# Dummy products on TensorE in three waits of a streaming encoder layer

## The chip, the cores and the metric

The kernel runs on one core of one Trainium2 chip, as one launch. The metric is the device time of the launch in microseconds (us); lower is better. The chip's other cores are idle.

## The reference, cut to what matters

One post-LN encoder layer is computed for 256 prompt frames and 64 sample frames together (320 tokens, model width 1024, float32). Cut to the branch in which the change lies:

```python
z = x @ w_in
q, k, v, u, vs, ga, gb = jnp.split(z, SPLIT_POINTS, axis=-1)
# A: chunked attention, 8 heads x 64, learned relative bias
sc = einsum('bnqhd,bnkhd->bhqk', q, k) * (A_HEAD_DIM ** -0.5) + bias
pr = jax.nn.softmax(sc, axis=-1)
oa = einsum('bnhqk,bnkhd->bnqhd', pr, v)
# B: spatial gating, 8 groups x 64 channels over 128-position chunks
un = jax.nn.gelu(u)
vn = layer_norm(jax.nn.gelu(vs), mlp_ln_g, mlp_ln_b)
ob = un * (tril(w_s[g]) @ vn + b_s[g])
mix = jax.nn.sigmoid(ga) * (oa @ w_branch_a) + jax.nn.sigmoid(gb) * (ob @ w_branch_b)
x = layer_norm(ALPHA * x + mix @ w_out, ln1_g, ln1_b)
# then 64 routed experts (top 8) and a shared one, a second norm, a gated embedding
```

## The kernel before

The kernel is written engine by engine: each engine has its own list of instructions, in the order in which the source has them, and semaphores tie the lists together. There is no planner; what an engine does next is what stands next in its list, and a wait holds back all that stands behind it on that engine.

The stages in order of time are: the input norm; the input projection in tiles of 128 columns (`products`, L1340, run by the loops of `project`); token-major copies, scores and softmax in between; the mixing product of branch B (L1418); the turned probabilities and the attention of branch A; the branch products with `w_branch_a` and `w_branch_b`, then with `w_out` (all L1340 again); the transposed result (L1493), the embedding product (`embed`, L1500), the first norm and the router; the routed experts in 16 steps of four experts (L1593, L1609, L1564, L1623); and the second norm and the output gate (L1704 to L1728).

The place of the change is the stretch between the last input projection and the first branch product. There TensorE's list reads:

- The mixing products (L1418): 24 products into PSUM banks 0 to 3; the last raises `mix_ps`.
- A wait for `prob_ready` 3, which VectorE raises after it has divided the last group of probabilities (L1007).
- `turn_probs(0)`: 12 transposes (L1426, L1428, L1431, L1434) into banks 4 to 6; the last raises `probT_ps`.
- A wait for `mix_ready` 1, which VectorE raises after it has read the mixing products from banks 0 to 3, added the bias rows (L1035, L1038) and multiplied by the activated `u` (L1040). `turn_probs(1)` writes banks 0 to 2, so it may not start before.
- `turn_probs(1)`: 12 transposes.
- `attend(0)`: its waits are `probT_act` 1 (ScalarE's copy of banks 4 and 5, L699) and `probT_dve` 1 (VectorE's copies of bank 6, L1049 and L1050); then 12 products (L1450 to L1460) into bank 7. Between `attend(0)` and `attend(1)` stands `turn_probs(2)`, behind `attend(1)` stands `turn_probs(3)`, and `attend(2)` and `attend(3)` follow. `attend` of an odd pair writes bank 3.
- A wait for `oa_ready` 4 (VectorE, L1054, after ScalarE's L705), and then the branch products.

SyncE's list has one gate in this stretch: it waits for `oa_ps` 4, which the last `attend` raises, before it loads the embedding's weights (L456 to L458) and, behind those, expert weights and the next pieces of the weight ring.

`ident` is the 128 x 128 identity in float32 that the transposes use. Bank 7 is written and read in earlier stages, and by `attend(0)` and `attend(2)`.

Of the kernel before, what the change touches and what calls it, by code (L numbers as in the profile page):

```python
# [34 lines left out]
P = 128  # L35
# [11 lines left out]
def trunk_step(nc, x_prompt, x_sample, cache_k, cache_v, p_prompt, p_sample, ln_in_g, ln_in_b, w_in,  # L47
# [30 lines left out]
    with ExitStack() as ctx:  # L78
        def sb(name, shape, dt=F32):
            return ctx.enter_context(nc.sbuf_tensor(name, shape, dt))  # L80
# [22 lines left out]
        ident = sb("ident", [P, P])  # L103
# [18 lines left out]
        PS = ctx.enter_context(nc.psum_tensor("PS", [P, 8, 512], F32))  # L122
# [1187 lines left out]
        def _(pe):  # L1310
# [67 lines left out]
            for h in range(HEADS):  # L1378
                par, i = h % 2, h // 2
# [20 lines left out]
            for w in range(2):  # L1400
                if w:
                    pe.wait_ge(score_ready, 4)
                for h in range(4 * w, 4 * w + 4):
                    par, i = h % 2, h // 2
                    for c, (key, n) in enumerate(((ckT[64 * par:64 * par + 64, i, :], 256), (head(K0, h, slice(256, TOK)), DH))):
                        ins = pe.matmul(PS[0:DH, 4 + 2 * par + i % 2, 256 * c:256 * c + n], query(h, 2), key,
                                        start=True, stop=True)
# [6 lines left out]
            for t in range(3):  # L1414
                n = ROWS[t]
                for g in range(8):
                    par = slice(64 * (g % 2), 64 * (g % 2) + 64)
                    ins = pe.matmul(PS[par, g // 2, cols(t)], vn[0:n, t, 64 * g:64 * g + 64], wsT[0:n, g, 0:n],  # L1418
                                    start=True, stop=True)
            ins.then_inc(mix_ps, 1)  # L1420

            def turn_probs(j):
                b = 4 if j % 2 == 0 else 0
                for e in range(2):
                    h = 4 * e + j
                    pe.transpose(PS[:, b + e, 0:P], prob0[:, h, :], ident[:, :])  # L1426
                    for c in range(2):
                        pe.transpose(PS[:, b + e, P * (c + 1):P * (c + 2)], prob1[:, h, P * c:P * (c + 1)], ident[:, :])  # L1428
                for e in range(2):
                    for c in range(2):  # L1430
                        pe.transpose(PS[:, b + 2, 192 * e + 64 * c:192 * e + 64 * c + 64], probs[:, 4 * e + j, P * c:P * (c + 1)],  # L1431
                                     ident[0:DH, 0:DH])
                for e in range(2):
                    ins = pe.transpose(PS[0:DH, b + 2, 192 * e + 128:192 * e + 192], probs[:, 4 * e + j, 256:TOK], ident[0:DH, 0:DH])  # L1434
                ins.then_inc(probT_ps, 1)

            def attend(j):
                pe.wait_ge(cache_loaded, 32)
                pe.wait_ge(probT_act, j + 1)
                pe.wait_ge(probT_dve, j + 1)  # L1440
                bank = 7 if j % 2 == 0 else 3
                if j >= 2:
                    pe.wait_ge(oa_ready, j - 1)

                for product in range(6):
                    for e in range(2):
                        rows, c, o = slice(64 * e, 64 * e + 64), slice(64 * (2 * j + e), 64 * (2 * j + e) + 64), 192 * e
                        pt, ps = probT[:, j, e, :], probT[:, j, 2, :]
                        if product == 0:
                            pe.matmul(PS[rows, bank, 0:P], v_tok[:, 0, c], pt[:, backwards(0, P)], start=True, stop=True)  # L1450
                        if product == 1:
                            pe.matmul(PS[rows, bank, P:2 * P], v_tok[:, 0, c], pt[:, backwards(P, 2 * P)], start=True, stop=False)
                        if product == 2:
                            pe.matmul(PS[rows, bank, P:2 * P], v_tok[:, 1, c], pt[:, backwards(2 * P, 3 * P)], start=False, stop=True)
                        if product == 3:
                            pe.matmul(PS[rows, bank, 256:TOK], cv[:, 0, c], ps[:, backwards(o, o + 64)], start=True, stop=False)
                        if product == 4:
                            pe.matmul(PS[rows, bank, 256:TOK], cv[:, 1, c], ps[:, backwards(o + 64, o + 128)], start=False, stop=False)
                        if product == 5:
                            ins = pe.matmul(PS[rows, bank, 256:TOK], v_tok[0:DH, 2, c], ps[0:DH, backwards(o + 128, o + 192)], start=False, stop=True)  # L1460
                ins.then_inc(oa_ps, 1)

            pe.wait_ge(prob_ready, 3)
            turn_probs(0)
            pe.wait_ge(mix_ready, 1)
            turn_probs(1)
            for j in range(4):
                attend(j)
                if j < 2:
                    turn_probs(j + 2)  # L1470
# [52 lines left out]
            for k in range(KD):  # L1523
                for wp, xp in ((0, 0), (0, 1), (1, 0)):
                    at = (wp * KD + k) * NE
                    ins = pe.matmul(PS[:, 6, 0:TOK], marks[:, at:at + P], xT[:, xp, k, :], start=(k == 0 and (wp, xp) == (0, 0)),  # L1526
                                    stop=(k == KD - 1 and wp == 1))
# [250 lines left out]
```

## Time and profile before

| | |
|---|---|
| time, median of 3 runs | 872.2 us (872.04 to 872.93) |
| the profiled execution's own time | 874.54 us |
| its span, first to last instruction | 872.5 us |
| TensorE (PE) busy | 819.9 us, 94% of the span |
| VectorE (DVE) busy | 381.5 us, 44% |
| ScalarE (ACT) busy | 269.1 us, 31% |
| chain that ended last | PE 86%, DVE 6%, DMA 3%, ACT 2% |
| mean granted TensorE clock | 0.986 of full speed |

The profile has one row for each group of instructions. A product of float32 operands shows as two records on PE and two weight loads on PEld; a transpose shows as one of each.
### The profile page before, as it was taken

The page shows a single profiled execution, that of the slowest core. Times are in us where ns is not written, and L with a number is a line of the kernel's source. Part 1 is how long each engine was busy: PE and PEld are TensorE (multiplying, and loading weights), DVE is VectorE, ACT ScalarE, POOL GpSimd, SP SyncE. Part 2 cuts the span into 40 slices and gives each one's busy share as a digit, 9 for nine tenths or more (in the row PEclk, how much of TensorE's full clock was granted, in tenths as well). Part 3 has the DMA queues.
Part 4 walks back from the last instruction along what each step waited for, and adds up shares of the span by engine and source line. Part 5 has one row for each costly group of instructions (what it writes and reads, how often), then busy time and mean ns, then how long its engine had stood idle before and what let it go on. Part 6 is the DMA issues. An engine that isn't in the chain of part 4 may idle for free.

```text
span 872.5 us, 13427 instructions
## 1 busy us (share of the span) xinstructions
PE 819.9 (94%) x4927; PEld 565.9 (65%) x4927; DVE 381.5 (44%) x846; ACT 269.1 (31%) x501; POOL 33.3 (4%) x50
## 2 busy tenths in 40 slices
PE   3999899889888999999999999999999999998887
PEld 2999799779877845555554654644645555553577
DVE  6435575737557834234224314414413423422674
ACT  2334466733434532211211211210220221120443
POOL 2001100000000320000000000000000000000000
PEclk9999999979999999999999999999999999999989
DMA  7596424427763059999999999999999999999001
GB/s 229 173 257 191 157 97 144 163 100 260 290 200 145 1 225 423 388 383 411 398 384 383 423 387 380 424 385 382 425 387 383 423 386 385 411 396 363 13 1 60
DMA packets 66041, 249.01 MB, mean 285 GB/s; under 512 B 5856, under 2 KB 37040, under 8 KB 41440
## 3 DMA queue, kind: packets, MB, share of 16 engines
q1 hardware_dynamic: 64848, 244.70, 71.3%
q0 software_dynamic: 1152, 3.95, 1.6%
q8 instruction: 16, 0.26, 0.1%
q14 instruction: 9, 0.07, 0.0%
q10 hardware_dynamic: 16, 0.02, 0.0%
HBM read 245.62 MB, written 3.03 MB: 285 GB/s over the span
## 4 chain that ended last, share of the span: by engine, by line
PE 86%; DVE 6%; DMA 3%; ACT 2%; SPq 1%; issue 1%; ACTq 0%; PEldq 0%; DVEq 0%
PE PS L1593 26%; PE PS L1340 20%; PE PS L1609 13%; PE PS L1623 9%; PE PS L1564 9%; PE PS L1714 4%; DMA weight_ring<-in_w_in_dram 1%; DMA weight_ring<-in_shared_w_dram 1%; PE PS L1602 1%; DVE xs L903 1%; PE PS L1572 1%; DMA expert_ring<-in_ln_in_b_dram 1%; PE PS L1526 1%; DVE xs L913 1%; DVE parts L1184 1%
## 5 line engine op out<-in xcount | busy, mean ns | idle before, releaser
L1593 PE MATMUL PS<-expert_ring,z 128*64 128x512 f32 x1024 | 223.7, 594 | 0.7 <-DVE z L1228 0.7
L1340 PE MATMUL PS<-parts,split 128*128 128x320 f32 x1344 | 202.3, 313 | 5.5 <-DVE parts L1068 3.3
L1340 PEld LDWEIGHTS PS<-parts,split 128*128 128x128 f32 x1344 | 200.4, 191 | 6.8 <-PEq L1483 3.5
L1593 PEld LDWEIGHTS PS<-expert_ring,z 128*64 128x64 f32 x1024 | 72.1, 137 | 139.7 <-issue 139.4
L1609 PE MATMUL PS<-expert_ring,z 128*64 128x512 f32 x512 | 113.7, 596 | 0.8 <-ACT z L788 0.8
L939 DVE TENSOR_TENSOR split<-weight_ring,split 128x512 fp32r<-128x512 f32 x106 | 73.8, 705 | 90.6 <-ACT split L635 90.3
L1224 DVE TENSOR_TENSOR split<-PS,split 128x512 fp32r<-128x512 f32 x64 | 44.3, 692 | 142.3 <-ACT split L793 141.9
L635 ACT ACTIVATE split<-weight_ring 128x512 fp32r<-128x512 f32 x112 | 69.9, 631 | 114.6 <-PE PS L1340 98.5
L784 ACT ACTIVATE z<-PS 128x256 f32<-128x256 f32 x32 | 12.3, 384 | 277.0 <-PE PS L1593 277.0
L1211 DVE SCALAR_TENSOR_TENSOR z<-PS,z 128x256 f32<-128x256 f32 x32 | 15.5, 485 | 183.1 <-ACT z L784 183.1
L1564 PEld LDWEIGHTS PS<-marks,parts 128*128 128x128 f32 x640 | 78.7, 191 | 14.0 <-issue 13.8
L1564 PE MATMUL PS<-marks,parts 128*128 128x256 f32 x640 | 85.0, 287 | 0.0
L1623 PEld LDWEIGHTS PS<-marks,split 128*128 128x128 f32 x512 | 75.2, 188 | 14.1 <-issue 13.0
L1623 PE MATMUL PS<-marks,split 128*128 128x320 f32 x512 | 80.5, 314 | 0.0
L1609 PEld LDWEIGHTS PS<-expert_ring,z 128*64 128x64 f32 x512 | 34.6, 136 | 66.2 <-issue 65.9
L793 ACT ACTIVATE split<-PS 128x512 fp32r<-128x512 f32 x64 | 38.2, 598 | 81.3 <-PE PS L1609 81.3
L1228 DVE TENSOR_TENSOR z<-z,PS 128x320 f32<-128x320 f32 x128 | 54.3, 484 | 11.7 <-PE PS L1623 10.1
L769 ACT ACTIVATE z<-PS 128x512 f32<-128x512 f32 x64 | 38.2, 597 | 47.8 <-PE PS L1564 47.8
L1714 PE MATMUL PS<-parts,split 128*128 128x320 f32 x192 | 31.9, 329 | 5.9 <-DVE parts L1274 4.8
L1714 PEld LDWEIGHTS PS<-parts,split 128*128 128x128 f32 x192 | 30.9, 205 | 6.7 <-issue 5.3
L1314 PE MATMUL PS<-ident,xs 128*128 128x128 f32 (+1 forms) x48 | 7.8, 326 | 15.7 <-DVE xs L913 15.7
L1165 DVE TENSOR_TENSOR marks<-z 128x256 fp32r<-128x256 f32 x51 | 18.6, 420 | 6.5 <-PE PS L1564 6.0
(225 smaller groups left out, 526.0 us busy)
## 6 DMA issues: line engine op xcount, KB each, us to landing
expert_ring<-in_exp_w_dram SPq DMA_DIRECT2D x192, 1024.0 KB, 10.0
weight_ring<-in_w_in_dram SPq DMA_DIRECT2D x36, 512.0 KB, 4.4
weight_ring<-in_w_out_dram SPq DMA_DIRECT2D x8, 512.0 KB, 4.4
expert_ring<-in_ple_w_gate_dram SPq DMA_DIRECT2D x2, 2048.0 KB, 10.2
weight_ring<-in_w_branch_a_dram SPq DMA_DIRECT2D x4, 512.0 KB, 3.6
weight_ring<-in_w_branch_b_dram SPq DMA_DIRECT2D x4, 512.0 KB, 4.6
weight_ring<-in_shared_w_dram SPq DMA_DIRECT2D x4, 512.0 KB, 7.2
xs<-in_x_prompt_dram SPq DMA_DIRECT2D x2, 512.0 KB, 4.5
```

The costliest lines, as they stand in the source:

```text
L635: nc.scalar.activation(split[:, 2 * (place % 2) + half, 0, :].rearrange("p (k n) -> p k n", k=4), raw, ACT.Copy)\
L769: nc.scalar.activation(xgT[:, 2 * g:2 * g + 2, :].rearrange("p k s -> p (k s)"), PS[:, g % 2, :], ACT.Copy)\
L793: nc.scalar.activation(ysplit[:, j, 0, 512 * half:512 * half + 512], PS[:, 5 + half, :], ACT.Copy)\
L939: nc.vector.tensor_tensor(parts[:, 1, :, :], raw, parts[:, 0, :, :].bitcast(F32), ALU.subtract).then_inc(w_low, 1)
L1224: nc.vector.tensor_tensor(ysplit[:, j, 1, c], PS[:, 5 + half, :], ysplit[:, j, 0, c].bitcast(F32), ALU.subtract).then_inc(y_low, 1)
L1228: nc.vector.tensor_tensor(accT[:, q, :], accT[:, q, :], PS[:, SCAT_BANK[q], 0:TOK], ALU.add)\
L1340: ins = pe.matmul(out, w[:, wp, :], xT[:, xp, k0 + k, :], start=(start and k == 0 and (wp, xp) == (0, 0)), stop=(stop and k == 3 and wp == 1))
L1564: ins = pe.matmul(PS[:, g % 2, 256 * k:256 * k + 256], xrows[:, part, t, 2 * g + k, :], pick[:, t, :], start=(t == 0 and part == 0), stop= ...
L1593: ins = pe.matmul(PS[c, 2 + j, :], xgT[:, k, P * j + 64 * e:P * j + 64 * e + 64], w13(j, e, k), start=(k == 0), stop=(k == KD - 1))
L1609: ins = pe.matmul(PS[c, 5 + half, :], hidT[:, j, k, c], w2(j, e, k, half), start=(k == 0), stop=(k == 1))
L1623: ins = pe.matmul(PS[:, SCAT_BANK[q], 0:TOK], ysplit[:, j, part, P * q:P * (q + 1)], scat[:, j, 0:TOK], start=(j == 0 and part == 0), stop ...
L1714: ins = pe.matmul(PS[:, tile % 2, 0:TOK], w[:, wp, :], xT[:, xp, k, :], start=(k == 0 and (wp, xp) == (0, 0)), stop=(k == KD - 1 and wp == 1))
```

## The change

A helper `fill(n)` puts n products into TensorE's list, each of which multiplies the identity by itself into the first 128 columns of PSUM bank 7. They wait for nothing, raise no semaphore, and nothing reads what they leave there: `attend(0)`, the next writer of that bank, starts its sums afresh. Four stand ahead of the wait for `prob_ready`, seven between `turn_probs(0)` and the wait for `mix_ready`, and five between `turn_probs(1)` and `attend(0)`, whose own waits follow. No wait is removed, added or moved, and the lists of the other engines are the same.

```diff
                 ins.then_inc(oa_ps, 1)
 
+
+            def fill(n):
+                for i in range(n):
+                    pe.matmul(PS[:, 7, 0:P], ident[:, :], ident[:, :], start=True, stop=True)
+
+            fill(4)
             pe.wait_ge(prob_ready, 3)
             turn_probs(0)
+            fill(7)
             pe.wait_ge(mix_ready, 1)
             turn_probs(1)
+            fill(5)
             for j in range(4):
                 attend(j)
                 if j < 2:
```

## Rows read from the trace of the kernel before

**Rows 1.** The page's 40 equal slices of the span: granted TensorE clock in tenths.

```profile
PEclk9999999979999999999999999999999999999989
```

**Rows 2.** Stretches: length, busy (records) of PE, PEld, DVE, ACT, POOL; PE clock; DMA.

```profile
172.30:175.70 3.40, 1.78 (x18) 1.33 (x18) 2.03 (x4) 2.90 (x3) 0.00 (x0) 1.00 0.28 97
175.70:179.10 3.40, 1.33 (x13) 1.32 (x14) 2.49 (x5) 1.31 (x2) 0.00 (x0) 0.51 0.00 0
179.10:182.50 3.40, 3.40 (x30) 2.66 (x28) 0.49 (x1) 0.44 (x1) 0.00 (x0) 0.50 0.00 0
182.50:185.90 3.40, 3.40 (x30) 3.14 (x30) 1.10 (x3) 1.25 (x2) 0.00 (x0) 0.50 0.02 5
185.95:190.78 4.83, 3.34 (x56) 2.74 (x55) 1.60 (x4) 1.69 (x3) 0.00 (x0) 1.00 0.11 14
```

**Rows 3.** Timeline of PE: start, length, instruction, records, idle before and its releaser.

```profile
168.10 2.58 PE L1418 MATMUL PS<-expert_ring 128*64 128x128 f32 x48 [1.20 <-ACT z L676]
171.37 0.33 PE L1426 MATMUL PS<-ident,expert_ring 128*128 128x128 f32 x1 [0.69 <-DVE expert_ring L1007]
...
172.47 0.27 PE L1434 MATMUL PS<-ident,expert_ring 64*64 64x64 f32 x2
174.36 0.33 PE L1426 MATMUL PS<-ident,expert_ring 128*128 128x128 f32 x1 [1.62 <-DVE z L1040]
...
177.81 0.70 PE L1450 MATMUL PS<-expert_ring 128*64 128x128 f32 x4 [2.07 <-DVE expert_ring L1050]
...
180.13 0.47 PE L1426 MATMUL PS<-ident,expert_ring 128*128 128x128 f32 x1
...
182.43 0.69 PE L1450 MATMUL PS<-expert_ring 128*64 128x128 f32 x4
...
184.74 0.47 PE L1426 MATMUL PS<-ident,expert_ring 128*128 128x128 f32 x1
...
186.43 0.27 PE L1434 MATMUL PS<-ident,expert_ring 64*64 64x64 f32 x2
186.63 0.44 PE L1450 MATMUL PS<-expert_ring 128*64 128x128 f32 x4
...
187.93 0.44 PE L1450 MATMUL PS<-expert_ring 128*64 128x128 f32 x4
...
190.78 3.49 PE L1340 MATMUL PS<-parts,split 128*128 128x320 f32 x22 [1.49 <-PEq L1473]
```

**Rows 4.** Timelines of DVE and ACT: what the waits of this stretch are for.

```profile
168.50 2.82 DVE L1007 TENSOR_TENSOR expert_ring<-expert_ring,srec 64x2560 f32<-64x2560 f32 x1
172.82 1.49 DVE L1040 TENSOR_TENSOR z<-expert_ring,z 128x1280 f32<-128x1280 f32 x1
177.39 0.27 DVE L1050 COPY expert_ring<-PS 64x128 f32<-64x128 f32 x1
175.52 1.49 ACT L699 ACTIVATE expert_ring<-PS 128x768 f32<-128x768 f32 x2
```

**Rows 5.** Chain of the end, two pieces: float32 products of full height, start and length.

```profile
270.71 1.08 PE PS L1500 x4
817.13 4.32 PE PS L1704 x16
```

**Rows 6.** Timeline of PEld: one load of 128 columns at the full clock.

```profile
171.37 0.14 PEld L1426 LDWEIGHTS PS<-ident,expert_ring 128*128 128x128 f32 x1 [0.82 <-DVE expert_ring L1007]
```

**Rows 7.** Timeline of SyncE's queue: the first load behind the gate on `oa_ps`.

```profile
189.34 0.37 SPq L456 DMA_DIRECT2D expert_ring<-in_ple_w_proj_dram  x1
```

**Rows 8.** Stretches elsewhere, columns as in rows 2: two lower-clock ones and two beside them.

```profile
222.50:223.45 0.95, 0.95 (x7) 0.95 (x8) 0.95 (x3) 0.25 (x1) 0.95 (x7) 1.00 0.68 248
223.50:226.85 3.35, 3.35 (x15) 3.35 (x14) 2.33 (x6) 0.63 (x1) 0.35 (x2) 0.50 1.02 355
...
831.10:837.80 6.70, 5.88 (x22) 5.91 (x23) 5.64 (x12) 2.79 (x6) 0.00 (x0) 0.50 0.00 0
...
254.70:257.50 2.80, 2.80 (x26) 2.80 (x27) 2.10 (x3) 0.57 (x2) 1.28 (x1) 1.00 0.02 6
```

## The prediction

> **What bounds the kernel now.** TensorE is busy for 94% of the span and carries 86% of the chain that ended last, so nearly every microsecond is a matter of how fast it works and where it has to wait. The first view to read is the page's line of granted clocks: all of the span runs near full speed but for a few slices, and the lowest of them, the ninth, is the place of the change [rows 1]. The second is a table of stretches around that place: the clock is 1.00 until 175.70, 0.50 from there to 185.90, and 1.00 again from 185.95 [rows 2]. Ahead of the fall TensorE was busy for only 1.78 of 3.40 us; while the clock was low it was first idle and then busy without a gap for 6.80 us. The third view is TensorE's own timeline, which names the idle pieces: 0.69 us until the last probabilities are divided, 1.62 us until the mixing result is free, and 2.07 us until the turned probabilities of the first pair are copied [rows 3]. VectorE's and ScalarE's rows say that these three waits end with their work, not with TensorE's [rows 4]. So the waits themselves can't be shortened by anything that TensorE does. What can change is the clock at which `attend` and `turn_probs` run behind them, and from 177.81 on each of them follows the one before with no wait between.
>
> **What the low clock costs.** The same two routines stand in the timeline at both levels, so the price is a difference of starts [rows 3]. One `attend` at the full clock takes 187.93 - 186.63 = 1.30 us. `attend(0)` takes 180.13 - 177.81 = 2.32 and `attend(1)` 184.74 - 182.43 = 2.31, so they lose 1.02 and 1.01 us. One `turn_probs` at the full clock takes 172.47 - 171.37 = 1.10 to its last two transposes, and those take 186.63 - 186.43 = 0.20 until the next routine starts: 1.30. `turn_probs(2)` takes 182.43 - 180.13 = 2.30 and loses 1.00; `turn_probs(3)`, in which the clock rises, takes 186.63 - 184.74 = 1.89 and loses 0.59. The sum is 1.02 + 1.00 + 1.01 + 0.59 = 3.62 us. All of it lies on the path: the branch products at 190.78 wait for the last `attend` and its two copies.
>
> **What is late next if it goes.** With the full clock from 177.81 on, `turn_probs(2)` ends at 177.81 + 2.60 = 180.41 and `turn_probs(3)` at 183.01. `attend(2)` follows at 183.01 and `attend(3)` at 184.31. The latter needs ScalarE's copy of `turn_probs(3)`: two copies take 1.49 us [rows 4], one thus about 0.75, which ends near 183.9, 0.4 us ahead of need. So no copy becomes the bound, and the branch products start at 187.16. SyncE's loads behind the gate on `oa_ps` begin at 189.34, right behind the last `attend` [rows 7], and move with it; DMA is all but idle in this stretch (0.00 to 0.11 of its time from 175.70 on [rows 2]), so there is no backlog that would hold them.
>
> **What the dummies cost.** Sixteen products of 128 columns are added, that is 32 records. No row has such a product, so its price is bounded. From below: float32 products of full height pass at 1.08 / 4 = 0.27 us a record for 320 columns, in two different places [rows 5]. By columns that is 0.27 x 128 / 320 = 0.108 us a record, 0.22 us a product, with the weight load hidden. From above: if the load of 128 columns, 0.14 us [rows 6], were not hidden at all, a record would take 0.108 + 0.14 = 0.25 and a product 0.50 us. I take 0.22, because the transposes are the nearest rows in shape, and theirs pass at 1.10 / 10 = 0.11 us each, load included [rows 3]. Nothing excludes a little more; a price below the bound of the stream has no row that would support it.
>
> With a price p the order of TensorE's list gives 170.68 + 4p for the end of the first four, if they start only where the mixing row ends (168.10 + 2.58). Then come 1.30 for `turn_probs(0)`, 7p, 1.30 for `turn_probs(1)`, and 5p. At p = 0.22 the first four end at 171.56, 0.19 us behind the release at 171.37; the seven at 174.40, 0.04 behind the release at 174.36; the five at 176.80, 1.01 us ahead of the release at 177.81. So `attend(0)` starts where it did, and the dummies cost nothing: VectorE and ScalarE, whose work ends the waits, hide them. What is queued behind them on TensorE is `turn_probs(0)` and `turn_probs(1)`; those are needed by ScalarE's copies at 175.52 and about 176.27, and would now end at about 172.9 and 175.7. The cover is used up where 170.68 + 2.60 + 16p = 177.81, at p = 0.28. The whole gain is used up where it is 177.81 + 3.62, at p = 0.51. The upper bound of 0.50 would leave 181.28, a delay of 3.47 and a gain of 0.15.
>
> The page "TensorE: Matmul & The Clock Gate" of the Trainium skill has a rule that speaks for the upper bound (Part 3: Packing small matmuls, "What overlaps and what doesn't"): a weight load overlaps with running products only when they use different groups of rows, and the dummies all use all 128. By that rule the sum would be the 872.05 that the upper bound gives. The rows of float32 products don't bear it out: theirs use all rows too, and 0.27 us leaves little room for a load of 0.14 beside the stream [rows 5, 6].
>
> **Whether they hold the clock.** This is the step that no row settles. For it: the fall came behind a stretch that was about half idle [rows 2], and with the dummies TensorE's idle time between 168.10 and 177.81 shrinks from 0.69 + 1.62 + 2.07 = 4.38 us to about 1.0. Against it: being busy is not enough in itself. From 179.10 to 182.50 TensorE was busy without a gap, with much of it transposes, and the clock did not rise; from 182.50 to 185.90, with more of `attend` in it, it did [rows 2, 3]. The dummies are products, like `attend`, not transposes, and they are asked to hold a clock, not to raise it; 2.80 us of transposes alone passed at 1.00 elsewhere [rows 8].
>
> **The rivals.**
>
> The dummies don't hold the clock. Then the five run at half speed, 5 x 0.44 = 2.20 us from 175.70 to 177.90, 0.09 us too late: 872.3. A milder form is a fall a little later, in the second half of the routines, that gives back part of the 3.62: 870.6 to 872. The page just named has a rule for that (Part 4: PE-mode transpose): transposes don't count as activity in the same way. The trace agrees in part: the transposes from 179.10 on did not raise the clock, but those at 254.70 kept it. Chance 0.11.
>
> More is gained than the sum. The kernel falls to the lower level in other places, and the moment isn't tied to an instruction: one fall comes at 223.50, after TensorE has been at work again for the 0.95 us from 222.50 [rows 8]. If the work arrives there 3.6 us earlier, a fall can be missed or shortened. The first costs 3.35 / 2 = 1.7 us, the second 5.88 / 2 = 2.9 us, of which about half might go: 865.3 to 867. Chance 0.16.
>
> The same chance of timing works the other way: a new fall, above all around 254.70, where transposes stand on the path behind a wait. Doubling the first eight of 24 costs about 1 us, all of them 2.80 us: 869.6 to 871.4, centre 870.9. Chance 0.06.
>
> Slower than before: the dummies don't pass in a stream, load and product of each record take turns. That is 0.14 + 0.33 = 0.47 us a record by single rows [rows 3, 6], 0.94 a product. `attend(0)` would start at 170.68 + 2.60 + 16 x 0.94 = 188.3, 10.5 us late, and the sum is 872.2 + 10.5 - 3.6 = 879.1. It decides from p = 0.51, and shows as over 0.2% from p = 0.62. Every run of float32 products in the trace speaks against it. Chance 0.03.
>
> **How the numbers follow.** The profiled execution took 874.54 us for a span of 872.5, 2.3 us more than the median of the timed runs, so the sum is 874.54 - 3.62 = 870.9 for such an execution, and 872.2 - 3.62 = 868.6 against the median. That is the forecast, with a chance of 0.64. The range of 865.5 to 871.2 takes in the rival with more gain, nearly all of the one with a new fall and a dummy price of up to 0.44 us; it leaves out the dummies that hold nothing and the slower case. A measurement of this kernel can tell about 0.2%, 1.7 us, from no change. Faster by more than that are the forecast and the larger gain, 0.80; within it the rivals of no hold and of a new fall, 0.17; slower 0.03.
>
> **What would show it.** In the profile of the changed kernel: a clock of 1.00 from 172 to 187; all four `attend` at 1.30 us and `turn_probs` at 1.30; a row of dummies at 0.11 us a record; `attend(0)` still released by L1050 near 177.8; the branch products near 187.2, and the chain behind them earlier by the same amount. The prediction is wrong if the clock still falls before 187, if the dummies' row reaches beyond 177.8, or if the falls of rows 8 come elsewhere or last longer.

## The result, and the profile after

The changed kernel is slower: 877.56 us (median of 8 runs, 874.53 to 880.84) against 872.88 us (869.93 to 874.81, 8 runs), a ratio of 1.005 with a 95% interval of 1.0026 to 1.0074. The profiled execution took 876.47 us for a span of 874.5 us, against 874.54 and 872.5 before. Forecast were 868.6 us and a range of 865.5 to 871.2. Ratios and medians are of executions within 1.5% of the fastest of their kernel; one alone was slower than that, of the kernel with 224 waits below (892.96 us).

In the stretch of the change the trace shows what was predicted. TensorE's timeline of the changed kernel there (columns as in rows 3; L1466 is the line of the dummies):

```profile
169.06 1.16 PE L1466 MATMUL PS<-ident 128*128 128x128 f32 x8
170.06 0.27 PE L1426 MATMUL PS<-ident,expert_ring 128*128 128x128 f32 x1
...
171.30 1.83 PE L1466 MATMUL PS<-ident 128*128 128x128 f32 x14
172.97 0.27 PE L1426 MATMUL PS<-ident,expert_ring 128*128 128x128 f32 x1
...
174.22 1.38 PE L1466 MATMUL PS<-ident 128*128 128x128 f32 x10
176.25 0.44 PE L1450 MATMUL PS<-expert_ring 128*64 128x128 f32 x4 [0.66 <-DVE expert_ring L1050]
...
177.55 0.33 PE L1426 MATMUL PS<-ident,expert_ring 128*128 128x128 f32 x1
...
178.85 0.44 PE L1450 MATMUL PS<-expert_ring 128*64 128x128 f32 x4
...
180.15 0.33 PE L1426 MATMUL PS<-ident,expert_ring 128*128 128x128 f32 x1
...
182.75 0.44 PE L1450 MATMUL PS<-expert_ring 128*64 128x128 f32 x4
185.61 6.57 PE L1340 MATMUL PS<-parts,split 128*128 128x320 f32 x43 [1.49 <-PEq L1481]
```

`attend` and `turn_probs` take 1.30 us each from start to start, and `attend(0)` is still released by VectorE's copy, now after 0.66 us of idle time instead of 2.07. From `attend(0)` to the branch products there are 185.61 - 176.25 = 9.36 us; before there were 190.78 - 177.81 = 12.97 [rows 3]. The gain is 3.61 us.

The whole stretch ran at the full clock, which the first row of this table of stretches shows (columns as in rows 2). The other rows are for later:

```profile
172.00:187.00 15.00, 12.86 (x162) 11.31 (x161) 6.49 (x14) 6.33 (x10) 0.00 (x0) 1.00 0.11 31
...
783.30:788.90 5.60, 0.00 (x0) 0.00 (x0) 1.68 (x5) 0.00 (x0) 0.00 (x0) 0.68 1.02 418
789.00:792.00 3.00, 3.00 (x8) 1.02 (x10) 0.00 (x0) 0.00 (x0) 0.00 (x0) 0.50 0.24 96
218.80:222.00 3.20, 3.20 (x14) 3.20 (x13) 1.85 (x4) 0.63 (x1) 0.00 (x0) 0.50 1.06 383
249.50:252.80 3.30, 3.16 (x15) 3.16 (x16) 1.72 (x2) 0.75 (x3) 1.27 (x1) 0.50 0.00 0
833.20:839.80 6.60, 5.95 (x22) 5.98 (x23) 5.59 (x12) 2.62 (x5) 0.00 (x0) 0.50 0.00 0
```

The loss is 600 us further on. The chain of the end, in the changed kernel, where the loop over the expert steps ends and the last step begins (start, length, what; "issue" is time in which the engine waited for nothing that the profile shows):

```profile
782.74 0.50 DVE z L1228
783.24 5.76 issue
788.99 15.53 PE PS L1601 x64
```

The same place in the kernel before:

```profile
787.92 0.50 DVE z L1228
788.42 0.19 issue
788.61 13.97 PE PS L1593 x64
```

The changed kernel arrives 787.92 - 782.74 = 5.18 us earlier. 3.61 us of that are the change. The rest was there ahead of it: `attend(0)` starts at 176.25 instead of 177.81, because the first 144 projection products took less time in this execution (first line) than in the one before (second line):

```profile
21.90 21.39 PE PS L1340 x144
21.76 23.10 PE PS L1340 x144
```

Then TensorE stands still for 5.76 us instead of 0.19, which takes back 5.57. The clock falls during that stand [the rows of 783.30 and 789.00 above], and the products behind it take 15.53 instead of 13.97 us, another 1.56. The balance is -5.18 + 5.57 + 1.56 = +1.95 us, the difference of the two spans.

While TensorE stands, no semaphore is waited for. What the DMA queues moved in those 5.6 us (packets, MB, share of 16 engines):

```profile
q1 hardware_dynamic: 315, 2.32, 100.4%
q8 instruction: 1, 0.02, 1.1%
```

The packet of 16 KB on q8 is an instruction fetch. In the trace the packets of that queue come 12 times up to about 370 us, none during the remaining 13 rounds of the loop, and then at 786.2 and 790.1 us; in the kernel before, at 791.4 and 794.9, behind the restart at 788.6 and not ahead of it. In both the first of them comes about 3 us behind the end of the loop (783.24 and 788.42).

### The profile page after: what moved, and what is told of

Same layout as the page of the kernel before. It is cut to its first block, busy times and chain, and to the rows that moved or that the text cites. A ratio compares the mean times of both kernels' runs of the same rounds, so it can differ in the third digit from the quotient of the medians.

```text
span 874.5 us, 13491 instructions
## 1 busy us (share of the span) xinstructions
PE 819.6 (94%) x4959; PEld 564.9 (65%) x4959; DVE 381.6 (44%) x846; ACT 268.8 (31%) x501; POOL 33.3 (4%) x50
## 4 chain that ended last, share of the span: by engine, by line
PE 87%; DVE 5%; ACT 2%; DMA 2%; issue 2%; SPq 1%; ACTq 0%; PEldq 0%; DVEq 0%
PE PS L1601 26%; PE PS L1340 20%; PE PS L1617 13%; PE PS L1631 9%; PE PS L1572 9%; PE PS L1722 4%; DMA weight_ring<-in_w_in_dram 1%; PE PS L1610 1%; DMA expert_ring<-in_ln_in_b_dram 1%; PE PS L1580 1%; DVE xs L903 1%; DVE xs L913 1%; DVE parts L1184 1%; PE PS L1508 1%; PE PS L1716 1%
```

## The experiments

**The theory.** TensorE's loop over the expert steps (391 instructions) is followed by a conditional block for overflow rounds, which these inputs never run; it is jumped over. By the built program's counts the code behind the jump begins 403 instructions behind the loop's last one. If instructions come in blocks, it matters in which block that code begins. The 16 dummies are 64 instructions (two loads and two products each), all ahead of the loop, and move everything behind by 64. Theory A: they push the code behind the jump across the edge of a block, into one that has not been fetched. Theory B: the stall comes with the dummies at work, or with arriving earlier.

The Trainium skill has this mechanism in "Runtime: NRT & Kernel Launch" (Instruction fetch mechanics): instructions are refilled in blocks of 16 KiB, 256 of them, in sequence, and a branch whose target is outside of what is loaded waits for a fetch. The trace agrees on the size of a block (packets of 16 KB) and has a fetch in the stand of 5.76 us.

**Never-executed instructions alone.**

```diff
             with pe.If(more > 0):
+                for _ in range(128):
+                    pe.wait_ge(const_ready, 1)
                 with pe.Fori(0, more) as r:
```

Two such waits make one instruction, so these are 64, in the block that is jumped over.

> The kernel before, with 64 instructions added inside TensorE's list in the conditional block that is jumped over behind the expert loop; they are never executed. Theory A (place of the code: the jump behind the expert loop lands in a 16 KB instruction block that has not been fetched when the code behind it lies 64 instructions further on): the stall of the changed kernel appears at the end of the expert loop, 5.8 us against 0.2 us, with a low clock behind it that costs about 1.5 us more, so about 872.9 + 7 = 880 us; the low clock around 176 to 186 stays as in the kernel before. Theory B (the stall comes from the dummies at work or from arriving earlier at the end of the loop): nothing that is executed has changed, so 872.9 us and no stall.

Measured: 880.34 us, ratio 1.0082 (1.0065 to 1.0098). The chain at the end of the loop:

```profile
783.35 5.57 issue
788.92 15.80 PE PS L1593 x64
```

Nothing that runs was changed, and the kernel is 7.2 us slower (873.16 beside it). The two lines account for it: (5.57 - 0.19) + (15.80 - 13.97) = 7.2 us. Dummies at work can't be the cause. This execution arrived as early as the changed kernel, so its trace alone doesn't exclude the other half of theory B; two traces below do, one that arrives at 794.40 and stands, and one that arrives at 782.14 and doesn't.

**The same 64 at the head.** The waits stand ahead of the first transposes, and are executed.

> The kernel before, with 64 waits on a semaphore that has long been raised put at the head of TensorE's list, where it idles for 16 us before the first norm; no dummies. Theory A: all code behind lies 64 instructions further on, as in the changed kernel, so the stall of about 5.8 us appears behind the expert loop: about 880 us, with the low clock around 176 to 186 kept. Theory B: 872.9 us, no stall.

Measured: 881.08 us, ratio 1.0098 (1.0073 to 1.0122), and a stall at the same place, as theory A has it:

```profile
784.17 5.75 issue
```

The jump here is as long as in the kernel before, so its length is not what counts.

**Moving the code on by 224 instead.** 160 waits at the head of the changed kernel, and 224 at the head of the kernel before.

> The changed kernel, with 160 waits on a raised semaphore at the head of TensorE's list, so that with the 64 instructions of the dummies all code behind lies 224 instructions further on than before; by the counts of instructions the jump behind the expert loop then ends in the block after the one it starts from, as in the kernel before. Theory A: no stall (0.2 us there), and the gain of the prediction is left: 872.9 - 3.6 = 869.3 us. Theory B: the stall stays, 877.6 us.

> The kernel before, with 224 such waits at the head and no dummies: the same place of all code as in the changed kernel with 160 waits. Theory A: no stall, 872.9 us as before, with the low clock around 176 to 186. A third theory (each added instruction on TensorE costs, wherever it lies): 224 instead of 64 added ones would give more than the 877.6 us of the changed kernel. The difference between this kernel and the changed kernel with 160 waits is the dummies alone: 3.6 us by the prediction's sum.

Measured: 875.82 us (ratio 1.0024, 1.0000 to 1.0049) and 885.72 us (1.0123, 1.0083 to 1.0163). Both expectations failed. The stall was there in both profiled executions, 5.80 and 5.76 us. A price for each added instruction (the third theory) doesn't fit either: with 160 more the changed kernel is not slower. In the kernel with 224 the waits at the head cost time by themselves, which shows as an idle piece ahead of the first products, so the difference between the two can't be read as the worth of the dummies:

```profile
18.52 8.05 issue
...
794.40 5.76 issue
```

The 12 times of the changed kernel with 160 waits lie in two groups, six from 871.5 to 873.9 us and six from 877.8 to 882.6. By the counts the loop there ends at most some 20 instructions behind the edge of a block. Whether the fetch that this sets off is at times made and at times not was argued, not shown; it stays open.

**Fewer instructions for the same dummies.** Products with 512, 512 and 384, and 512 and 128 columns in the three waits, 20 instructions in all.

```diff
-            def fill(n):
-                for i in range(n):
-                    pe.matmul(PS[:, 7, 0:P], ident[:, :], ident[:, :], start=True, stop=True)
+            def fill(*widths):
+                for n in widths:
+                    pe.matmul(PS[:, 7, 0:n], ident[:, :], k_tok[:, 0, 0:n], start=True, stop=True)
```

> The changed kernel with its 16 dummy products of 128 columns made into 5 of 512, 512, 384, 512 and 128 columns (the identity times rows of the attention keys): the same columns in each of the three waits, but 20 added instructions instead of 64. Theory A (place of the code): by the counts the code behind the jump still begins in the block after the last one of the loop, so no stall there (0.2 us), the clock stays at 1.00 between 172 and 187, and the gain of the prediction is left: 3.6 us, 872.9 - 3.6 = 869.3 us. Theory B (the dummies at work, or an earlier arrival, cause the stall): about 877.6 us, like the changed kernel.

Measured: 873.57 us, ratio 1.0025 (0.9998 to 1.0052), with single times from 869.2 to 879.4. The profiled execution, 869.22 us, has no stall at the jump and a small one later:

```profile
782.14 0.21 issue
782.35 4.93 PE PS L1601 x21
787.28 0.56 issue
787.84 9.67 PE PS L1601 x43
```

So the stall of the changed kernel is gone with the dummies at work and an early arrival, as theory A wants. But the median did not reach 869.3, and a gain of 3.6 us (a ratio of 0.996) lies outside the interval. The slower ones of its times have no trace, and what took the gain in them stays open.

> The kernel with the five wide dummies, and 44 instructions that are never executed in the conditional block that is jumped over, so that the code behind the jump lies 64 instructions further on than before, as in the changed kernel. Theory A: the stall of 5.8 us and the low clock behind it are back, about 877 us, as in the changed kernel; the clock between 172 and 187 stays at 1.00. Theory B: as the kernel with the wide dummies alone.

Measured: 878.68 us, ratio 1.0091 (1.0057 to 1.0126). Forty-four instructions that never run cost 878.68 - 873.57 = 5.1 us, and the stall is back:

```profile
785.18 5.87 issue
```

**How far from the edge.**

> The kernel before with 40 instead of 64 never-executed instructions in the block that is jumped over. Theory A, with the block's edge where the times of the instruction fetches put it (some 50 to 60 instructions behind the jump's target in the kernel before): 40 don't reach the edge, so no stall, 872.9 us. If it were the length of the jump and not the edge of a block: a good part of the 7 us that 64 instructions cost.

Measured: 878.7 us, ratio 1.007 (1.0047 to 1.0094). Not "no stall", but a shorter one, and not at the jump; the time is nearly that of 64 instructions all the same:

```profile
788.35 0.18 issue
788.53 2.78 PE PS L1593 x11
791.31 2.61 issue
793.93 13.45 PE PS L1593 x53
```

TensorE runs for 2.78 us behind the jump and then stands; the fetch begins at 791.3 us. My expectation lacked this: a landing shortly ahead of an edge leaves too little time for the next fetch. The profile accounts for 2.61 us of standing and 2.78 + 13.45 - 13.97 = 2.26 of low clock, 4.9 of the 6.4 us measured.

In the profiled executions the stall grows with the instructions added. With none added all 64 records behind the landing pass in one piece; the stand is 0.56 us at 20, 2.61 at 40, 2.62 at 44 (the next kernel), and 5.57 to 5.87 at 64 in the five kernels that have 64. Ahead of it 21, 11 and 10 records pass at 20, 40 and 44. From 20 to 40 that is ten records and their ten loads fewer, just the 20 instructions: the stall is tied to one place in the code, as an edge is. From the landing to the restart the three take 5.49, 5.40 and 5.40 us, whatever part of that is work. Whether 64 instructions put the landing just behind the edge or just ahead of it these runs don't tell, as TensorE would stand equally long.

**More dummies.** The wide ones, and dummies in four other idle pieces of TensorE: ahead of the first transposes, during the branch gates, ahead of the router's product, and between the second norm's products and the gate; 44 instructions ahead of the jump.

> The kernel with the five wide dummies, and dummies of 128 columns in four other idle pieces of TensorE: 14 in a loop ahead of the first transposes, 10 in a loop while the branch gates are worked off, 5 in a loop ahead of the router's product, 20 in the wait between the second norm's products and the gate. Together 44 instructions are added ahead of the jump, too few to reach the block's edge. Theory A with the clock as the reason of the gain: the falls at 223.5 (1.7 us), 274.7 (1.7 us) and 831.1 (2.9 us) go or shorten, and the first stage reaches the full clock earlier (up to 3 us): 860 to 866 us. If dummies only help where the prediction had them: 869.3 us.

Measured: 872.77 us, ratio 0.9996 (0.9970 to 1.0023), short of the 860 to 866 expected. The clock was at 1.00 from 27 to 785 us, and then comes a stall:

```profile
782.27 2.78 PE PS L1610 x10
785.05 2.62 issue
787.67 13.83 PE PS L1610 x54
```

**No jump.** The overflow rounds become rounds of the same loop, whose length is read ahead of it.

```diff
-            with pe.Fori(1, STEPS - 1) as i:
-                expert_step(i, 4 * i + 4)
-            more = pe.value_load(rounds_i[0:1, 0:1], min_val=0, max_val=MAX_ROUNDS - 1)
-            with pe.If(more > 0):
-                with pe.Fori(0, more) as r:
-                    with pe.Fori(0, STEPS) as i:
-                        expert_step(r * STEPS + i + STEPS - 1, 4 * i)
+            pe.wait_ge(rounds_ready, 1)
+            more = pe.value_load(rounds_i[0:1, 0:1], min_val=0, max_val=MAX_ROUNDS - 1)
+            with pe.Fori(1, more * STEPS + STEPS - 1) as i:
+                expert_step(i, (4 * i + 4) % NE)
             expert_step(more * STEPS + STEPS - 1, None, last=True)
```

> The kernel before, with TensorE's expert loop and its conditional overflow rounds written as one loop whose length is read ahead of it, so that no block of code is jumped over behind the loop. No dummies. Theory A (place of the code): the stall there was 0.2 us at the good place, so nothing is gained or lost: 872.9 us, low clock around 176 to 186 as before.

> The changed kernel with the same single loop: all 16 dummies and their 64 instructions, and no jump behind the loop. Theory A: no stall, so the dummies' own worth is left, 3.6 us against the kernel before with the single loop: 869.3 us. Theory B (the dummies or an earlier arrival cause the stall): 877.6 us as in the changed kernel.

Measured: 872.22 us without dummies (ratio 1.0005, 0.9982 to 1.0027) and 869.71 us with all 16 (0.9963, 0.9937 to 0.9989). The changed kernel without its jump has no stall; its chain goes from the loop to the last step in one piece:

```profile
784.53 4.95 PE PS L1631 x32
789.48 13.91 PE PS L1601 x64
```

The dummies, with their 64 instructions, are worth 872.22 - 869.71 = 2.5 us here; drawing anew from the twelve times of each puts 95% of such differences between 0.6 and 4.7 us, so 3.6 fits too.

> The kernel with wide dummies in the three waits and dummies in four other idle pieces, with the single loop. With them alone, and the jump, a stall of 2.6 us stood behind the loop. Theory A: no stall and no fall of the clock behind it: about 4 us below the 872.8 us it took with the jump, and two low stretches fewer than the kernel before: 863 to 868 us. If low clock is not what costs: no better than the changed kernel with the single loop.

Measured: 865.99 us (864.83 to 869.84), ratio 0.9934 (0.9909 to 0.9958): faster than both kernels, 7.1 us below the 873.13 of the kernel before in the same set. In its profiled execution, the slowest of the eight, the clock still fell at 23.2, 251.9 and 801.4 us. Three stretches in which the kernel before fell ran at the full clock. Two of those falls are in rows 8 (223.50, 831.10); the third is the first line here, from the kernel before:

```profile
274.70:278.05 3.35, 3.35 (x15) 3.35 (x14) 2.17 (x6) 0.00 (x0) 0.00 (x0) 0.50 1.00 423
```

```profile
219.00:228.00 9.00, 8.62 (x59) 8.65 (x60) 5.77 (x12) 3.85 (x8) 1.76 (x8) 1.00 0.75 270
272.00:279.00 7.00, 7.00 (x49) 6.72 (x49) 3.52 (x14) 1.06 (x2) 0.76 (x1) 1.00 1.00 415
825.00:840.00 15.00, 13.52 (x97) 12.70 (x96) 13.45 (x24) 8.55 (x16) 0.00 (x0) 1.00 0.00 1
```

**The clock by itself, at the same place of all code.** The dummies replaced by as many waits that are already fulfilled:

```diff
             def fill(n):
-                for i in range(n):
-                    pe.matmul(PS[:, 7, 0:P], ident[:, :], ident[:, :], start=True, stop=True)
+                for i in range(8 * n):
+                    pe.wait_ge(const_ready, 1)
```

> The changed kernel with each dummy product replaced by as many instructions that only look at a semaphore raised long ago: 64 instructions in the same three places, so all code lies where it does in the changed kernel, and TensorE's array is idle in the waits as before. The stall behind the loop stays, about 5.8 us. The clock falls around 176 as in the kernel before. If the prediction's sum for the clock is right, this is 3.6 us slower than the changed kernel: 881 us; if the dummies are worth nothing, 877.6 us.

Measured: 881.24 us, ratio 1.0098 (1.0063 to 1.0132). That is 881.24 - 877.56 = 3.7 us above the changed kernel, where 3.6 were expected. The two were timed in different sets (the kernel before took 873.13 and 872.88), and drawing anew from their six and eight times puts 95% of such differences between 0.6 and 5.8 us: that the dummies gain is shown, and how much rests on the traces. The stall is 5.75 us, and the clock falls as before:

```profile
177.40:187.50 10.10, 8.60 (x68) 7.33 (x69) 3.48 (x9) 2.40 (x5) 0.00 (x0) 0.50 0.01 2
```

Its timeline shows what the low clock costs, 192.11 - 178.90 = 13.21 us instead of 9.36:

```profile
178.90 0.69 PE L1450 MATMUL PS<-expert_ring 128*64 128x128 f32 x4 [1.63 <-DVE expert_ring L1050]
...
192.11 2.17 PE L1340 MATMUL PS<-parts,split 128*128 128x320 f32 x13 [1.49 <-PEq L1481]
```

## Why the prediction was wrong

**What the low clock costs: right.** The sum was 3.62 us. The two traces give 3.61, and the pair at the same place of all code 3.7 in the timed runs, with the width said there.

**Whether the dummies hold the clock: right.** The granted clock was 1.00 from 172 to 187 with dummies, and 0.50 with waits in their place. In all seven traces with dummies, of either kind, it was 1.00 from the first dummies to the branch products; in all seven without it fell between 171 and 185 us.

**What is late next: right, but read too short.** No copy and no load became the bound, and the branch products start 3.6 us earlier. I followed the path to them and took it that all behind moves along. It did, as far as the end of the expert loop.

**What the dummies cost: the step that failed.** The step took the price of the dummies to be their time in TensorE's list, and found it hidden, so it put their cost at nothing. As time, it was: 14 records take 172.97 - 171.30 = 1.67 us, 0.119 a record and 0.24 a product, where I had 0.22 and the cover ended at 0.28. The step did not count them as code. Sixty-four instructions moved all that follows by a quarter of a block of 256, and the code behind a jump came to lie at the edge of a block or across it. That cost 5.57 us of standing and 1.56 of low clock in the profiled execution, and 7.2 us in the timed runs by 64 instructions that never run. With the 3.7 us gained, 7.2 - 3.7 = 3.5 us of loss are expected; 4.7 were measured, with single times of each kernel spread over 5 to 6 us.

**The rivals.** The slower side was given 0.03, for dummies that don't pass in a stream. They do. The Trainium skill's rule on weight loads ("TensorE: Matmul & The Clock Gate", Part 3), which was weighed for the upper bound, isn't borne out either: records that all use the same 128 rows passed at 0.119 us each, less than the 0.14 of a single load [rows 6]. The true slower case was on no list. It could have been seen: the list of queues on the profile's page before has one for instructions, with 16 packets of 16 KB, and TensorE's list has a block of some 400 instructions that is jumped over.

**More is gained elsewhere, or a new fall.** Both happened in this one execution: low stretches at 218.8, 249.5 and 833.2 [rows 8 for those before], of which the one at 249.5 is new, and 23.10 - 21.39 = 1.7 us less in the first stage. They come elsewhere in each execution, and were a reason to widen the range on both sides, not for a direction.

## What to carry to other kernels

An added instruction has two prices: its time on its engine, and its place in the code. Ahead of a loop that is left by a jump over code, even instructions that never run can cost several microseconds hundreds of microseconds later, so compare such an edit with one that adds as many idle instructions at the same place, or take the jump away first. Dummy products in idle pieces are worth what the low clock costs behind them, here 2.5 to 3.7 us in one stretch and 872.22 - 865.99 = 6.2 us in seven idle pieces, without the jump in both kernels.

## What the runs showed that was not expected

- A jump to code whose block is still to be fetched holds TensorE for 5.6 to 5.9 us while DMA is busy with other loads (418 GB/s in that stretch of the changed kernel). The low clock behind such a stand costs 1.4 to 2.8 us more: the 64 records behind it took 15.40 to 16.80 us in seven traces, against 13.97.
- Landing near the end of a loaded block costs too: 2.6 us of standing, 2.8 us behind the landing.
- The clock's falls differ between executions of one kernel: the kernel with wide dummies took from 869.2 to 879.4 us, and the profiled execution of its fastest time had no low stretch between 27 and 825 us.
